# Block two of a four-layer network: another order of projection units, selection rounds and scalings

## The chip, the cores and the metric

The kernel runs on one core of a Trainium2 chip. The metric is the device time of one execution in microseconds (us). TensorE (PE) does the matmuls, VectorE (DVE), ScalarE (ACT) and GpSimd (POOL) the elementwise work, and SyncE (SP) issues the weight loads. Each engine runs its own program in order; they meet only at semaphores.

## The reference

Two blocks of two layers each work on a residual stream of 512 tokens by 1024 channels, in float32. Block one (dilated attention and a gated delta rule, then a convolutional feed-forward) is not touched. A layer of block two computes:

```python
h = rms_norm_2(x, g_pre_mix[l])
u_pool, q, k, v, iq, ik, iw = jnp.split(h @ w_in[l], SPLIT_POINTS, axis=-1)
q, k, iq, ik = ...          # partial rotation (rope) of each
a_out = pool_mixer(u_pool, w_pool[l], pool_scale[l])
b_out = dsa_attention(q, k, v, iq, ik, iw, topk)      # topk = 128
x = x + rms_norm_2(jnp.concatenate([a_out, b_out], -1) @ w_out[l], g_post_mix[l])
h = rms_norm_2(x, g_pre_ffn[l])
x = x + rms_norm_2(jnp.square(jax.nn.relu(h @ w_ff1[l])) @ w_ff2[l], g_post_ffn[l])
```

The pool mixer takes, for four groups of 128 channels, the mean over the last 2, 4, 8 or 16 tokens minus the token itself, multiplies by a 128x128 matrix and scales by a factor per channel. The attention first scores every key for every query: eight index heads give `relu(iq . ik / 8)`, and the score is their sum weighted by `iw`. Only the 128 best keys of a query (among those allowed by 64-token chunks) take part in the softmax attention of eight heads of width 64.

## The kernel before

**Tiling.** Tokens are the free dimension (512), channels the partitions. Weights come as "units" of 128x1024 floats, which is one block of 128 output columns. SP loads a unit into one of two `raw` slots, ACT copies it to `wH` (rounded, `high_of`, line 977), POOL subtracts to get `wL` (`low_of`, line 788), and PE multiplies (`unit`, line 1961): for each of 8 channel tiles three matmuls (high by high, low by high, high by low), 24 matmuls of 128x512. `wH` and `wL` have two slots, so a unit can be prepared once the unit two before it is done.

**The projection stage of block two.** Each layer has `IN2` = 22 places: 0 is `ik`; 1 to 4 are the index queries `iq`; 5 to 8 the four pool groups; 9 and 10 two of the attention's `q` units; place 11 (`WPOOL`) is no unit but the loading of the pool matrices; 12 and 13 are the other two of `q`, 14 to 17 `k`, 18 to 21 `v`. Accumulators alternate between two PSUM banks.

- A unit of `ik`, `iq`, `q` or `k` is "turned" (numbered j = 0 to 12): ACT copies the accumulator out (`turn_input`, line 1083), PE multiplies the copy by a permutation after the next unit's matmuls (`turn`, line 2127), POOL multiplies the copy by the cosines (line 933), and DVE multiplies PE's result by the sines and adds (`turn_finish`, lines 1520 and 1524).
- A unit of `v` (j = 13 to 16) is transposed by PE (line 2131), and DVE scales the result per token into `v2` (line 1528).
- A pool unit is scaled by DVE into `pu` (line 1508), and `pool_window` (lines 1866 to 1875) adds shifted copies of it in one to four doubling steps (2, 4, 8, 16 tokens), partly in SBUF, the last in PSUM bank `SC[1]`, which odd turns use too. ACT and POOL split the result into `pdH` and `pdL` (lines 1018 and 824).
- `pool_mix` (lines 2164 to 2166) multiplies the windows by the pool matrices: groups 0 and 1 at `WPOOL`, 2 and 3 one place later. It writes the banks that odd index pairs use, so it waits until the scores of 14 pairs are taken in. `pool_scaled` on DVE (line 1856) then scales them into `piece`, and ACT and POOL split that.

**Index scores.** Sixteen pairs of heads (128, 256, 384 and 512 keys wide, four pairs each) are spread by `IX_AT` over the places. `index_logits` (line 2115) issues a pair between the channel tiles of a unit, the last pair before the last tile. ACT applies relu in place (line 1330), DVE multiplies by the head's weight and adds into `bias2` (`index_score`, lines 1814 and 1816). There are two sets of two banks, so PE's pair n waits until DVE has taken in pair n-2; pairs 14 and 15 share one set, so 15 waits for 14.

**Selection.** `top_round` finds the eight largest scores of each query and removes them: a MAX8 (line 1830) and a MATCH_REPLACE8 (line 1833) for each token tile, 16 rounds for each of tiles 1, 2 and 3. `TOP_AT` says which rounds run on DVE at the end of which place, `TOP_STEPS` which run between the 35 steps of the attention. A round needs nothing but the scores.

**Attention.** Step n: PE multiplies k by q (line 2222), DVE adds the selection bias and finds the maximum (line 1542), ACT takes the exponential (line 1092), PE transposes (line 2234) one step later. Between them `FILL` puts matmuls of the output projection (`half_step`, lines 2190 to 2192), two steps of three matmuls ahead of every second transposition.

DVE's loop over the places is written out: at place u it does the scaling of a pool unit, the scores of the pairs issued at place u+1, the turn or window of u, and then the rounds of u. ACT's loop: the relus of u, `turn_input`, the weight copy for u+2, then the pieces. POOL's loop: the weight subtraction for u+2, the cosines, then the pieces.

## Time and profile before

| | |
|---|---|
| median of three runs | 2760.77 us (2760.47 to 2763.85) |
| the profiled execution | 2765.85 us, of which the traced span is 2764.1 us |
| PE busy | 2685.1 us, 97% of the span |
| DVE, ACT, POOL busy | 1098.6, 1102.5, 1211.5 us (40, 40, 44%) |
| chain that ended last | PE 87%, DVE 5%, ACT 2%, issue 2%, DVE's sequencer 2%, POOL 1% |
| mean granted clock of TensorE | 0.990 |
| units of block two's first layer, from the turn after place 4 to the turn after place 14 | 1547.09 to 1621.24 us |
| the same of its second layer | 2168.30 to 2243.83 us |

The table reads so: PE is the engine that sets the time, and its idle time in the whole span is 79 us. The projection stage of block two ends, and its attention begins, at 1666 us in the first layer and at 2289 us in the second. What the change can move are the times at which PE waits there.

### The profile page before, as it was taken

To read this page: it belongs to the slowest core of one execution; us is meant where nothing else is said; L and a number is where in the kernel's file an instruction comes from. 1 tells how busy PE (TensorE), PEld (TensorE's weight loads), DVE (VectorE), ACT (ScalarE), POOL (GpSimd) and SP (SyncE) were. 2 spreads that over 40 slices of the span, in tenths; PEclk is the share of its full clock that TensorE was granted. 3 is DMA by queue.
4 is the path that set the end of the run, shared out by engine and by line. 5 is a ranking of instruction groups with operands and counts; after the bars stand their busy time and mean duration, and the time that the engine had idled before them with its cause. 6 is when DMAs were issued, how large, how long until landed. Compare 5 with 4: busy or idle time off the path is not lost.

```text
span 2764.1 us, 42821 instructions
## 1 busy us (share of the span) xinstructions
PE 2685.1 (97%) x15208; PEld 2112.3 (76%) x15208; DVE 1098.6 (40%) x2260; ACT 1102.5 (40%) x1871; POOL 1211.5 (44%) x630
## 2 busy tenths in 40 slices
PE   9999999999999999999999999999999999999997
PEld 7767777888877677788887666788888666788886
DVE  4455454441154553644402586510113586510112
ACT  4454254443345533544434235532333235532331
POOL 3323235555433232355544452464653452364653
PEclk9999999999999999999999999999999999999998
DMA  3211023333322100233232221133332221133332
GB/s 136 77 54 40 9 77 91 99 93 105 106 71 69 54 25 24 78 97 96 94 106 92 71 69 47 62 99 99 92 98 84 71 69 47 61 97 94 99 93 97
DMA packets 62867, 217.16 MB, mean 79 GB/s; under 512 B 6576, under 2 KB 6704, under 8 KB 62480
## 3 DMA queue, kind: packets, MB, share of 16 engines
q1 hardware_dynamic: 62416, 214.28, 24.7%
q8 instruction: 83, 1.36, 0.2%
q0 software_dynamic: 320, 1.12, 0.2%
q14 instruction: 48, 0.39, 0.0%
HBM read 213.28 MB, written 2.10 MB: 78 GB/s over the span
## 4 chain that ended last, share of the span: by engine, by line
PE 87%; DVE 5%; ACT 2%; issue 2%; DVEq 2%; POOL 1%; DMA 0%; ACTq 0%; SPq 0%; POOLq 0%
PE bank L1961 61%; PE bank L2337 3%; PE bank L2011 3%; PE bank L2190 2%; PE bank L2191 2%; PE bank L2192 2%; PE bank L2023 1%; PE bank L2222 1%; PE bank L2234 1%; PE bank L2245 1%; PE bank L2127 1%; PE bank L1995 1%; PE bank L2356 1%; DVE mT L1786 1%; PE bank L1988 1%
## 5 line engine op out<-in xcount | busy, mean ns | idle before, releaser
L788 POOL TENSOR_TENSOR wL<-raw,wH 128x1024 fp32r<-128x1024 f32 x371 | 893.1, 2408 | 1085.5 <-ACT wH L977 1085.4
L1961 PE MATMUL bank<-hH,wH 128*128 128x512 f32 x1680 | 679.8, 405 | 7.0 <-DVE mT L1786 4.2
L1961 PE MATMUL bank<-hL,wH 128*128 128x512 f32 x1680 | 657.9, 392 | 0.0
L1961 PE MATMUL bank<-hH,wL 128*128 128x512 f32 x1680 | 657.5, 391 | 0.0
L977 ACT ACTIVATE wH<-raw 128x1024 fp32r<-128x1024 f32 x371 | 392.2, 1057 | 531.1 <-PE bank L1961 490.8
L1961 PEld LDWEIGHTS bank<-hH,wH 128*128 128x128 f32 x1680 | 317.1, 189 | 102.4 <-issue 28.8
L1961 PEld LDWEIGHTS bank<-hH,wL 128*128 128x128 f32 x1680 | 317.3, 189 | 67.5 <-issue 6.0
L1961 PEld LDWEIGHTS bank<-hL,wH 128*128 128x128 f32 x1680 | 316.9, 189 | 67.8
L1961 PE MATMUL bank<-hidH,wH 128*128 128x512 f32 x864 | 336.7, 390 | 0.0
L1961 PE MATMUL bank<-hidH,wL 128*128 128x512 f32 x864 | 336.2, 389 | 0.0
L1961 PE MATMUL bank<-hidL,wH 128*128 128x512 f32 x864 | 336.1, 389 | 0.0
L1919 DVE SCALAR_TENSOR_TENSOR relu<-bank,rstd 128x512 f32<-128x512 f32 x64 | 44.1, 691 | 458.2 <-PE bank L1961 449.5
L1961 PEld LDWEIGHTS bank<-hidH,wH 128*128 128x128 f32 x864 | 162.2, 188 | 35.8 <-issue 1.6
L1961 PEld LDWEIGHTS bank<-hidL,wH 128*128 128x128 f32 x864 | 162.2, 188 | 33.7
L1961 PEld LDWEIGHTS bank<-hidH,wL 128*128 128x128 f32 x864 | 162.2, 188 | 33.1
L824 POOL TENSOR_TENSOR hidL<-piece,hidH 128x512 f32 (+1 forms) x108 | 139.8, 1295 | 92.8 <-ACT hidH L1018 75.5
L1786 DVE SCALAR_TENSOR_TENSOR mT<-bank,par,mT 128x511 f32<-128x511 f32 (+1 forms) x176 | 131.9, 750 | 115.8 <-ACT mT L1289 101.7
L1092 ACT ACTIVATE sc<-sc,st 128x128 f32<-128x128 f32 (+3 forms) x128 | 71.7, 560 | 109.2 <-DVEq L1545 109.0
L1782 DVE TENSOR_TENSOR bank<-bank,rstd 128x512 f32<-128x512 f32 x88 | 61.5, 698 | 118.2 <-PE bank L1961 110.8
L1463 DVE TENSOR_TENSOR mT<-mT,bank 128x512 f32<-128x512 f32 x42 | 28.9, 687 | 160.5 <-PE bank L1961 128.0
L2190 PE MATMUL bank<-hH,wH 128*128 128x512 f32 (+1 forms) x208 | 81.2, 390 | 1.1 <-POOL hL L824 1.1
L2192 PE MATMUL bank<-hL,wH 128*128 128x512 f32 (+1 forms) x208 | 77.8, 374 | 0.0
(378 smaller groups left out, 3629.9 us busy)
## 6 DMA issues: line engine op xcount, KB each, us to landing
raw<-w_dram SPq DMA_DIRECT2D x398, 512.0 KB, 3.5
x<-x_dram SPq DMA_DIRECT2D x4, 512.0 KB, 9.6
out_dram<-x SPq DMA_DIRECT2D x1, 2048.0 KB, 6.3
const<-const_dram SPq DMA_DIRECT2D x1, 1229.0 KB, 13.2
par_next<-par_dram POOLq DMA_DIRECT2D x5, 168.0 KB, 3.5
qkT<-pos_dram POOLq DMA_DIRECT2D x1, 256.0 KB, 7.3
const<-const_dram SPq DMA_DIRECT2D x1, 131.0 KB, 2.2
```

The lines of the kernel that those rows point to most:

```text
L788: pool.tensor_tensor(wL[:, s, :], raw[:, s, :], wH[:, s, :].bitcast(F32), ALU.subtract).then_inc(w_lo.sem, 1)
L824: pool.tensor_tensor(dst, shape(src), hi.bitcast(F32), ALU.subtract).then_inc(piece_lo.sem, 1)
L977: act.activation(wH[:, s, :], raw[:, s, :], ACT.Copy).then_inc(w_hi.sem, 1)
L1092: act.activation(sc[:, n % 2, 0:wd], sc[:, n % 2, 0:wd], ACT.Exp, bias=st[:, MN + n % 4:MN + n % 4 + 1], scale=-1.0, accum_out=st[:, SUM + ...
L1782: dve.tensor_tensor(banks[s][:, :], banks[s][:, :], rstd[:, :], ALU.mult).then_inc(acc_scaled.sem, 1)
L1786: last = dve.scalar_tensor_tensor(buf[:, lag:S], banks[s][:, 0:S - lag], prmd(w, "fconv", i * 12 + 6 * q + 3 * s + 2 - lag), buf[:, lag:S] ...
L1961: mm = pe.matmul((out or ACC[bk])[:, :], wt[:, c:c + P], rhs, start=first and k == 0 and j == 0, stop=last and k == tiles - 1 and j == 2)
L2011: pe.matmul(out[u][:, :], wt[:, k * P:k * P + P], hH[:, k, :], start=k == 0 and j == 0, stop=False)
L2190: pe.matmul(out[:, cols], wH[:, p % 2, c:c + P], high[:, cols], start=k == 0, stop=False)
L2191: pe.matmul(out[:, cols], wL[:, p % 2, c:c + P], high[:, cols], start=False, stop=False)
L2192: mm = pe.matmul(out[:, cols], wH[:, p % 2, c:c + P], low[:, cols], start=False, stop=k == 3)
L2337: mm = pe.matmul(o, *two, start=True, stop=True)
```

## The change

It renumbers the places of block two. The four pool groups sit at places 5, 7, 9 and 11, between them and at 12 the `q` units (6, 8, 10, 12), and `WPOOL` becomes 13. The sixteen index pairs are dealt two to a place (6 to 12, and 14) where they were 2, 3, 3, 3, 3 and 2 (6 to 10, and 12). The rounds of `TOP_AT` are dealt anew, with the same number for each tile. Scaling the pool results goes from DVE (one instruction and ACT's copy) to ACT (two instructions, one for `piece`, one for `pdH`), and scaling the values goes from DVE (one instruction of 128x512) to ACT (four of 128x128). Odd turns from j = 5 wait for the windows finished up to their place. The SP queue issues the same loads; only their order follows the places.

```diff
@@ -65,14 +65,19 @@
 GROUPS = (28 + 16 + 2 * NJ + KD, 21 + 16 + NH2 + KD * FCHUNKS)
 
 
-WPOOL, IN2, HALF_A, HALF_B, FF_2 = 11, 22, 22, 26, 30
+POOLS = (5, 7, 9, 11)
+WPOOL, IN2, HALF_A, HALF_B, FF_2 = 13, 22, 22, 26, 30
 G_HALF, G_FF2 = (28, 21), 37
 HALF_OF = ((28, 32), (HALF_A, HALF_B))
 
 
 def tensor_of(p):
 
-    return p if p < WPOOL else IN2 - 1 if p == WPOOL else p - 1
+    if p in POOLS:
+        return 5 + POOLS.index(p)
+    if p == WPOOL:
+        return IN2 - 1
+    return p if p < 5 else p - 1 if p > WPOOL else 9 + sum(q < p for q in range(5, p) if q not in POOLS)
 
 
 def group_of(b, u):
@@ -186,15 +191,17 @@
 
 
 IX_AT, _y = {}, 0
-for _u, _n in ((6, 2), (7, 3), (8, 3), (9, 3), (10, 3), (12, 2)):
+for _u, _n in ((6, 2), (7, 2), (8, 2), (9, 2), (10, 2), (11, 2), (12, 2), (14, 2)):
     IX_AT[_u] = tuple(range(_y, _y + _n))
     _y += _n
 assert _y == 16
 
 
-TOP_AT = {10: [[1, 2]], 11: [[1, 2, 3], [1, 2, 3]]}
-for _u in range(12, IN2 - 2):
-    TOP_AT[_u] = [[1, 2, 3]] + ([[1]] if 13 <= _u < 18 else [[2]] if _u >= 18 else [])
+TOP_AT = {9: [[1]], 10: [[1, 2]], 12: [[1, 2]], 13: [[1, 2]], 18: [[1, 2, 3], [1, 2, 3]]}
+for _u in range(14, 18):
+    TOP_AT[_u] = [[1, 2, 3], [1]]
+for _u in (19, 20):
+    TOP_AT[_u] = [[1, 2, 3], [2, 3]]
 TOP_STEPS = {1: [[2]], 3: [[2]], 5: [[3]], 7: [[2]], 9: [[3]], 11: [[3]], 13: [[3]], 15: [[3]], 17: [[3]]}
 _done = {1: 0, 2: 0, 3: 0}
 for _table in (TOP_AT, TOP_STEPS):
@@ -666,13 +673,13 @@
 
             if b == 0:
                 return u if u < 12 else None
-            if u < POOL_U:
-                return u
-            return None if u < POOL_U + 4 or u == WPOOL else u - 4 - (u > WPOOL)
+            if u in POOLS or u == WPOOL:
+                return None
+            return u - sum(p < u for p in (*POOLS, WPOOL))
 
         def unit_of_turn(b, j):
 
-            return j if b == 0 or j < POOL_U else j + 4 + (j + 4 >= WPOOL)
+            return j if b == 0 else [u for u in range(IN2) if turn_of(1, u) is not None][j]
 
         def acc_of(w, u):
 
@@ -932,8 +939,8 @@
                         pool.wait_ge(turn_done.sem, turn_done.at(w, j - 1))
                         pool.tensor_tensor(pt2[:, j % 2, :], turn_src(1, j), rope_r(1)[0],
                                            ALU.mult).then_inc(cos_done.sem, 1)
-                    if 0 < u - POOL_U <= 4:
-                        g = u - POOL_U - 1
+                    if u - 1 in POOLS:
+                        g = POOLS.index(u - 1)
                         piece_low(w, N_PD2 + g, piece[:, g % 2, :], pdL[:, g, :], pdH[:, g, :])
                     if u in (WPOOL + 1, WPOOL + 2):
                         for g in (0, 1) if u == WPOOL + 1 else (2, 3):
@@ -1108,6 +1115,29 @@
                 if w.b and n in HIGHS_AT:
                     f = HIGHS_AT[n]
                     piece_high(w, N_ATT2 + f, piece[:, f % 2, :], att_place(w, f, hH), heads)
+
+            def pool_scaled(w, g):
+
+                if g == 1:
+                    act.wait_ge(unit_done.sem, unit_done.at(w, WPOOL + 1))
+                else:
+                    act.wait_ge(pool_done.sem, pool_done.at(w, (1, 0, 2, 3)[g]))
+                act.wait_ge(piece_ready.sem, piece_ready.at(w, N_PY2 + g))
+                act.wait_ge(piece_lo.sem, piece_lo.at(w, N_PY2 + g - 1))
+                act.activation(piece[:, g % 2, :], MIX[g % 2][:, :], ACT.Copy,
+                               scale=prm(w, "pscale", g, g + 1)).then_inc(piece_ready.sem, 1)
+                act.activation(pdH[:, g, :], MIX[g % 2][:, :], ACT.Copy,
+                               scale=prm(w, "pscale", g, g + 1)).then_inc(piece_hi.sem, 1)
+
+            def value_scaled(w, j):
+
+                f = j - N_ROT[1]
+                act.wait_ge(turn_done.sem, turn_done.at(w, j))
+                act.wait_ge(turned.sem, turned.at(w, j + 1))
+                for t in range(NT):
+                    last = act.activation(v2[:, t, f * P:f * P + P], turned_bank(1, j)[:, t * P:t * P + P], ACT.Copy,
+                                          scale=rtok[:, t:t + 1])
+                last.then_inc(turn_done.sem, 1)
 
             def first_half(w, h):
 
@@ -1336,12 +1366,15 @@
                         high_of(w, 4)
                     elif u >= 3:
                         high_of(w, u + 2)
-                    if 0 < u - POOL_U <= 4:
-                        g = u - POOL_U - 1
+                    if u - 1 in POOLS:
+                        g = POOLS.index(u - 1)
                         piece_high(w, N_PD2 + g, piece[:, g % 2, :], pdH[:, g, :])
-                    if u in (WPOOL + 1, WPOOL + 2):
-                        for g in (0, 1) if u == WPOOL + 1 else (2, 3):
-                            piece_high(w, N_PY2 + g, piece[:, g % 2, :], pdH[:, g, :])
+                    if u in (WPOOL, WPOOL + 1):
+                        for g in (0, 1) if u == WPOOL else (2, 3):
+                            pool_scaled(w, g)
+                    if u and (turn_of(1, u - 1) or 0) >= N_ROT[1]:
+                        value_scaled(w, turn_of(1, u - 1))
+                value_scaled(w, turn_of(1, IN2 - 1))
                 for n in range(SLOTS):
                     for h in HALVES_AT[n - 1] if n else ():
                         first_half(w, h)
@@ -1846,16 +1879,6 @@
                                   8 ** -0.5, None, ALU.mult)
                 dve.drain()
 
-            def pool_scaled(w, g):
-
-                if g == 1:
-                    dve.wait_ge(unit_done.sem, unit_done.at(w, WPOOL + 1))
-                else:
-                    dve.wait_ge(pool_done.sem, pool_done.at(w, (1, 0, 2, 3)[g]))
-                new_piece(w, N_PY2 + g)
-                dve.tensor_scalar(piece[:, g % 2, :], MIX[g % 2][:, :], prm(w, "pscale", g, g + 1), None,
-                                  ALU.mult).then_inc(piece_ready.sem, 1)
-
             def pool_window(w, g):
 
                 win = 2 << g
@@ -1886,20 +1909,14 @@
                         gate_scale(w)
                     j = turn_of(1, u)
                     if j is None and u != WPOOL:
-                        unit_scaled(w, u, pu[:, (u - POOL_U) % 2, :], acc_free[u % 2].sem)
+                        unit_scaled(w, u, pu[:, POOLS.index(u) % 2, :], acc_free[u % 2].sem)
                         dve.drain()
-                    if u == WPOOL:
-                        for g in (0, 1):
-                            pool_scaled(w, g)
                     for y in (2 * pair + h for pair in IX_AT.get(u + 1, ()) for h in range(2)):
                         index_score(w, y)
-                    if j is not None:
+                    if j is not None and j < N_ROT[1]:
                         turn_finish(w, j)
-                    elif u != WPOOL:
-                        pool_window(w, u - POOL_U)
-                    if u == WPOOL + 1:
-                        for g in (2, 3):
-                            pool_scaled(w, g)
+                    elif j is None and u != WPOOL:
+                        pool_window(w, POOLS.index(u))
                     for rounds in TOP_AT.get(u, ()):
                         top_round(rounds)
                 for n in range(SLOTS):
@@ -2119,8 +2136,9 @@
                 src, to = turn_src(w.b, j), turned_bank(w.b, j)
                 bk, a = acc_of(w, unit_of_turn(w.b, j))
                 pe.wait_ge(acc_free[bk].sem, acc_free[bk].at(w, a + 1))
-                if w.b and j == POOL_U:
-                    pe.wait_ge(piece_ready.sem, piece_ready.at(w, N_PD2 + 4))
+                if w.b and POOL_U <= j < 15 and j % 2:
+                    windows = sum(p < unit_of_turn(1, j) for p in POOLS)
+                    pe.wait_ge(piece_ready.sem, piece_ready.at(w, N_PD2 + windows))
                 if w.b and j == 15:
                     pe.wait_ge(ix_used.sem, ix_used.at(w, 32))
                 if j < N_ROT[w.b]:
@@ -2159,7 +2177,7 @@
                     pe.wait_ge(ix_used.sem, ix_used.at(w, 28))
                 pe.wait_ge(piece_lo.sem, piece_lo.at(w, N_PD2 + g + 1))
                 if g >= 2:
-                    pe.wait_ge(piece_ready.sem, piece_ready.at(w, N_PY2 + g - 1))
+                    pe.wait_ge(piece_hi.sem, piece_hi.at(w, N_PY2 + g - 1))
                 c = g * P
                 pe.matmul(MIX[g % 2][:, :], pwH[:, c:c + P], pdH[:, g, :], start=True, stop=False)
                 pe.matmul(MIX[g % 2][:, :], pwL[:, c:c + P], pdH[:, g, :], start=False, stop=False)
```

## Rows read from the trace of the kernel before

**Rows 1.** the page: busy time of each engine, share of the span.

```profile
PE 2685.1 (97%) x15208; PEld 2112.3 (76%) x15208; DVE 1098.6 (40%) x2260; ACT 1102.5 (40%) x1871; POOL 1211.5 (44%) x630
```

**Rows 2.** stretches: length, PE PEld DVE ACT POOL busy, clock, DMA share, GB/s.

```profile
1547.00:1609.00 62.00, 55.41 (x227) 34.64 (x226) 46.50 (x86) 22.26 (x47) 24.28 (x13) 0.97 0.21 67
...
1582.00:1588.00 6.00, 6.00 (x20) 4.06 (x18) 5.59 (x9) 1.31 (x3) 3.36 (x2) 0.72 0.23 79
```

**Rows 3.** PE's waits, each layer of block two: total, times, longest.

```profile
PE bank L2115 <- DVE bias L1816: 5.8, 4, 2.0
...
PE bank L2115 <- DVE bias L1816: 7.4, 4, 2.8
```

**Rows 4.** timeline of PE, first layer: start, length, instruction, idle before.

```profile
1547.09 1.02 PE L2127 MATMUL bank<-turn_in,const 128*128 128x512 f32 x2
...
1580.39 0.92 PE L2115 MATMUL bank<-ikT,iqT 64*128 64x384 f32 x4 [2.04 <-DVE bias L1816]
...
1595.72 0.47 PE L2164 MATMUL bank<-pdH,pwH 128*128 128x512 f32 x1 [0.76 <-issue]
...
1606.20 1.13 PE L2115 MATMUL bank<-ikT,iqT 64*128 64x512 f32 x4 [1.62 <-DVE bias L1816]
...
1621.24 1.02 PE L2127 MATMUL bank<-turn_in,const 128*128 128x512 f32 x2
```

**Rows 5.** timeline of PE, second layer.

```profile
2168.30 1.02 PE L2127 MATMUL bank<-turn_in,const 128*128 128x512 f32 x2
...
2213.29 1.88 PE L2115 MATMUL bank<-ikT,iqT 64*128 64x512 f32 x4 [2.78 <-DVE bias L1816]
...
2243.83 1.02 PE L2127 MATMUL bank<-turn_in,const 128*128 128x512 f32 x2
```

**Rows 6.** timeline, a DVE window step and a POOL instruction beside it.

```profile
1573.25 2.65 DVE L1866 TENSOR_TENSOR sc<-sc 128x510 f32<-128x510 f32 x1
...
1572.69 2.66 POOL L788 TENSOR_TENSOR wL<-raw,wH 128x1024 fp32r<-128x1024 f32 x1 [2.91 <-ACT wH L977]
```

**Rows 7.** DVE's groups by shape, 1540 to 1670 us: busy, mean ns.

```profile
L1816 DVE SCALAR_TENSOR_TENSOR bias<-bank,iw,bias 128x512 f32<-128x512 f32 x7 | 5.2, 750 | 2.3 <-ACT bank L1330 1.8
...
L1866 DVE TENSOR_TENSOR sc<-pu 128x511 f32<-128x511 f32 x3 | 2.1, 692 | 0.3
```

**Rows 8.** ACT's groups by shape, the same stretch.

```profile
L1018 ACT ACTIVATE pdH<-piece 128x512 fp32r<-128x512 f32 x8 | 5.0, 634 | 20.8 <-DVEq L1876 18.4 <-DVE piece L1856 2.3
...
L1330 ACT ACTIVATE bank<-bank 128x512 f32<-128x512 f32 x8 | 4.3, 577 | 9.0 <-PE bank L2115 9.0
```

**Rows 9.** timeline of PE, end of the projection and start of the attention.

```profile
1646.55 1.02 PE L2127 MATMUL bank<-turn_in,const 128*128 128x512 f32 x2
...
1666.15 0.49 PE L2222 MATMUL bank<-kT,qT 64*128 64x128 f32 x4
...
1668.07 0.27 PE L2234 MATMUL bank<-const,sc 128*128 128x128 f32 x1
```

**Rows 10.** timeline of DVE, rounds of the selection and the first softmax step.

```profile
1601.11 0.89 DVE L1830 MAX8 top<-bias 128x8 f32<-128x256 f32 x2
...
1603.24 1.41 DVE L1856 TENSOR_SCALAR piece<-bank,par 128x512 f32<-128x512 f32 x2
...
1649.16 1.48 DVE L1830 MAX8 top<-bias 128x8 f32<-128x256 f32 x3
...
1652.47 0.43 DVE L1830 MAX8 top<-bias 128x8 f32<-128x256 f32 x1
...
1653.53 0.69 DVE L1528 TENSOR_TENSOR v<-bank,rtok 128x512 f32<-128x512 f32 x1
...
1657.43 0.56 DVE L1830 MAX8 top<-bias 128x8 f32<-128x384 f32 x1
...
1666.88 0.29 DVE L1542 CUSTOM_DVE_ANT_0 sc<-bank,bias 128x128 f32<-128x128 f32 x1
```

**Rows 11.** timeline of ACT, the first exponential of the attention.

```profile
1667.25 0.40 ACT L1092 ACTIVATE sc<-sc,st 128x128 f32<-128x128 f32 x1 [0.80 <-DVEq L1545]
```

## The prediction

> **What bounds the kernel now.** First the page: PE is busy for 97% of the span [rows 1], so only PE's waits and its slow clock can be given back. Then the table of stretches [rows 2]: in the first layer's stretch with the pools and index scores (1547 to 1609 us) PE is busy 55.4 of 62 us at a granted clock of 0.97. The waits name the cause [rows 3]: PE waits for DVE's index scores four times a layer, 5.8 and 7.4 us. The timeline shows where [rows 4, 5]: at the third pair of a place (2.04 and 2.78 us) and at pair 15 (1.62 us). Right after the 2.04 us wait the granted clock is 0.72 for 6 us [rows 2], part of it at the lower of the two levels: (1-0.72) x 6 = 1.7 us lost. The 512 wide pair after the wait of 2.78 us takes 1.88 us instead of the 1.13 of another [rows 4, 5]. With the 0.76 us ahead of the first pool matmul [rows 4] and 0.1 at each restart, some 8.5 us are lost in the first layer (5.8 + 0.8 + 1.7), and 1.4 more in the second, by the lengths of the same work: 2243.83-2168.30 = 75.5 against 1621.24-1547.09 = 74.15 us. That is all that the reordering can give: some 18 us.
>
> **Stage A, places 5 to 14.** The work on PE is the same, so I follow the engines from the turn after place 4 (time 0). A place with its turn takes PE (1646.55-1621.24)/4 = 6.33 us [rows 4, 9], without it about 5.4 (the turn's 1.02 overlaps by 0.1), an index pair its duration and about 0.15. With two pairs a place no pair but 15 has to wait for the pair two before it: four waits a layer become one. But DVE gets a full queue. From place 10 on it holds, in order: the scores of pairs 8 and 9 (done at 39.1), the third window, one round of tile 1, the scores of 10 and 11, a round of two tiles (1603.24-1601.11 = 2.1 us [rows 10]), the finish of a turn (two of 0.69 and drains, 1.6), the scaling of the last pool group (0.8), the scores of pairs 12 and 13 (four of 0.75, 0.83 with their gaps [rows 7]).
>
> How long a window takes hangs on POOL. A step of a window adds two SBUF operands: 0.69 us alone [rows 7], 2.65 us where POOL's weight subtraction runs [rows 6]. The third window is 3.5 us clean (four operations and the ends), the fourth 4.35. In the new order each falls on a subtraction of 2.4 us and a cosine product of 1.3, which follow a `q` unit at once. I add 3.5 us to the third and 2.5 to the fourth (bounds: 0 and 3.7 each, all of both POOL instructions). The third then ends at 46.3, 0.8 us after PE wants it for its odd turn; DVE reaches pairs 12 and 13 at 54.85 and ends them at 58.15, while PE ends place 12 at 55.2: it waits 3 us ahead of the pool matmuls, where it waited 0.8. (If the third window takes 5.5 us, 2.2.)
>
> Next wait: pair 15, issued in place 14. The fourth window ends at 65.1. ACT has stood waiting for it and then does its piece (0.63 [rows 8]), the weight copy for place 15 (1.06), and the new scalings of two pool groups, four instructions at a pitch of about 0.5 (the relu of the same 512 columns is 0.58 [rows 8]); only then comes the relu of pair 14, and DVE adds two products of 0.83. Sum: 65.1 + 0.1 + 0.6 + 1.0 + 2.0 + 0.6 + 1.6 = 71.0. PE wants pair 15 at 66.6: 4.5 us of waiting, where it was 1.62. PE ends place 14 at 73.05. The same work (one turn more, two pool matmul groups less, 0.5 us) was done before at 1621.24-1547.09-0.5 = 73.65 us in the first layer and 2243.83-2168.30-0.5 = 75.05 in the second [rows 4, 5]. One low-clock stretch of up to 1.65 us after the long wait is to be added, so stage A gives -0.6 to +1.0 and -2.0 to -0.4: I take -1 us for both layers. With clean windows pair 15 comes 2.5 to 4 us earlier, -4 a layer; with POOL's full block +1.5.
>
> The rule for the block is in the Trainium skill, SBUF — State Buffer, section Who interferes with whom: a VectorE instruction with two SBUF inputs and a GpSimd instruction that reads SBUF exclude each other for the whole instruction, whichever comes first. The pair at 1573 us agrees: DVE 2.65 us, POOL 2.66 where it mostly takes 2.4. By the rule both POOL instructions hold the window up, which leads to the -1; if only running beside each other slowed them a little, it would be -4 a layer.
>
> **Stage B, the start of the attention.** The rounds are the same in number, but not in place. Before, DVE has at places 18 and 19 a three-tile and a one-tile round each; after, place 18 has two three-tile rounds, 19 and 20 each a three-tile and a two-tile one. None waits for anything, so DVE goes through them without a pause after the last `k` turn, and the attention's first step stands behind them. Durations [rows 10]: three tiles 1652.47-1649.16 = 3.3 us, tile 1 alone 1653.53-1652.47 = 1.06, tile 2 alone 1.28 (0.56, 0.54 and gaps), tiles 2 and 3 about 2.5 (three tiles less tile 1's 0.8). From DVE's start on place 17's rounds (1649.16, which is 2.6 us after PE's turn at 1646.55 [rows 9]): 4.35 for place 17, 6.6 for 18, 5.8 for 19, 5.8 for 20, and 0.6 to close tile 1 = 23.15 us, so DVE is free at 1672.3. The first softmax step was at 1666.88 [rows 10]: DVE is 5.4 us late. PE had 0.4 us of slack at its first transposition (1668.07 [rows 9], the exponential from 1667.25 to 1667.65 [rows 11]), and has nothing to fill with but the two steps already there; DVE's selection round behind step 1 takes away the rest of the slack. I take 5.4 us a layer (bounds: 4.9, if DVE works off the lag in its gaps, and 5.7). It cannot be shortened by PE's gain in stage A, since it counts from a turn that moves along.
>
> The wait is longer than any of [rows 4, 5], so a stretch at the low clock should follow: 0 to 1.7 us a layer by [rows 2], I take 1.2.
>
> The values: four ACT instructions of 128x128 a unit, about 0.85 us, instead of 0.69 on DVE. After the last unit ACT does a copy of its input, a weight copy and eight of these, some 3.4 us, until its first exponential. That hides behind DVE's lag; without the lag it would cost some 0.9 us a layer (from 1667.25, the first exponential, to 1668.1). ACT's doubled pool scalings delay place 17's weights to some 0.8 us before PE wants them: hidden, but nothing is left over. The waits of odd turns for four windows are met by then, and the SP queue brings each load a place earlier than needed: zero.
>
> **Sum.** -1 + 2 x 5.4 + 2 x 1.2 = +12.2 us. The profiled execution took 2765.85 us with a span of 2764.1; the median is 5.1 lower, 2760.77. I put the difference on the median: 2773.0 us.
>
> **Rivals.**
> 1. Stage A pays for stage B (no change). If the windows run clean, A gives -4 to -5 a layer and no low clock follows B: 2760.8 - 9 + 10.8 = 2762.6. For it: the windows at places 5 and 7 mostly fall between POOL's instructions. Against: the third and fourth start within a subtraction by my schedule. 0.13.
> 2. Faster: the third-pair waits go and nothing takes their place. Place and price: the 8.5 and 9.9 us of stage A less what remains of pair 15 (1.6 each): 2745.6. It decides at the point where the rounds of places 18 to 20 end: it needs them inside 17.7 us from 1649.16, and I count 23.15. 0.04; in between, a half of both (2755 or less) 0.03.
> 3. Slower still: POOL blocks all of both windows, the lag passes to the weights behind ACT's scalings (place 17 and 18, 1 us each), and each long wait has its low clock: 2760.8 + 3 + 10.8 + 6.8 = 2781. 0.13.
> 4. The moved scalings on ACT decide, not DVE's rounds: then PE's first waits of the attention name ACT's exponential after ACT's own queue, and the time is 2760.8 - 1 + 2 = 2762, within the same as rival 1. 0.03.
>
> The forecast holds 0.64. Its own range is 2767 to 2779; rivals 1 and 4 at 2762 and rival 3 near 2781 lie at the edges, so the range is 2763 to 2780. A measurement of this kernel can tell from no change what is over 0.2%, 5.5 us: slower (over 2766.3) 0.77, within 0.16 (rivals 1 and 4), faster 0.07 (rival 2).
>
> **What would show it.** In the profile after: no wait of PE for index scores in places 7 to 11; 2 to 3 us of waiting ahead of the first pool matmul and 2.5 to 5 at pair 15, behind ACT's pool scalings; one wait of about 5 us in each layer at the attention's first transposition, with DVE busy on MAX8 and MATCH_REPLACE8 until some 25.7 us after the last `k` turn; then a stretch of 0.6 us matmuls. The prediction is wrong if DVE reaches the first softmax step within a microsecond of PE's first product, or if stage A gains over 5 us a layer.

## The result, and the profile after

The changed kernel takes 2782.88 us (median of 5 runs, 2778.95 to 2788.58) against 2762.91 for the kernel before, measured alongside (2760.47 to 2767.95): ratio 1.0071, interval 1.006 to 1.0082. It is slower by 20.0 us. The forecast was 12.2 us more, 2773.0, in a range from 2763 to 2780: the direction is right, the step is 7.8 us too short and the time lies 2.9 us above the range.

The profiled execution took 2788.58 us, with a span of 2786.8, so 22.7 us more of span than before. It is the slowest of the five: 5.7 us above their median, at a mean granted clock of 0.985 where the other four have 0.987 to 0.989. What its rows say of the clock is therefore more than a usual execution loses. Its totals, against [rows 1] (busy time, share of the span, instructions):

```profile
span 2786.8 us, 42861 instructions
PE 2698.0 (97%) x15208; PEld 2121.7 (76%) x15208; DVE 1094.0 (39%) x2244; ACT 1116.8 (40%) x1911; POOL 1211.9 (43%) x630
```

The same 15208 matmuls are busy for 13 us more, at a mean granted clock of 0.985 where it was 0.990. The rest, some 10 us, is waiting. PE's waits over the whole span (total, times, longest):

```profile
PE bank L2252 <- ACT turn_in L1114: 11.0, 6, 2.6
PE bank L2252 <- ACT sc L1099: 10.8, 2, 5.6
...
PE bank L2182 <- issue: 5.6, 2, 2.8
PE bank L2132 <- DVE bias L1849: 4.6, 2, 2.3
```

The index-score waits of [rows 3], 13.2 us in 8 places, are down to 4.6 in 2. In their place stand two waits of 2.8 ahead of the pool matmuls (L2182) and two of over 5 us at the attention's first transposition (L2252 behind ACT's exponential, L1099). Where the 22.7 us are, by the timeline of PE (start, length, instruction, what it waited for; rows of both layers, compare [rows 4, 5, 9]):

```profile
1547.64 1.02 PE L2145 MATMUL bank<-turn_in,const 128*128 128x512 f32 x2
...
1593.61 1.10 PE L2145 MATMUL bank<-turn_in,const 128*128 128x512 f32 x2 [0.28 <-DVEq L1899]
...
1605.53 0.47 PE L2182 MATMUL bank<-pdH,pwH 128*128 128x512 f32 x1 [2.79 <-issue]
...
1618.04 1.13 PE L2132 MATMUL bank<-ikT,iqT 64*128 64x512 f32 x4 [2.30 <-DVE bias L1849]
...
1665.37 0.49 PE L2240 MATMUL bank<-kT,qT 64*128 64x128 f32 x4
...
1672.71 0.48 PE L2252 MATMUL bank<-const,sc 128*128 128x128 f32 x1 [5.26 <-ACT sc L1099]
...
1691.30 0.41 PE L2252 MATMUL bank<-const,sc 128*128 128x128 f32 x2 [2.60 <-ACT turn_in L1114]
...
2180.29 1.02 PE L2145 MATMUL bank<-turn_in,const 128*128 128x512 f32 x2
...
2299.53 0.49 PE L2240 MATMUL bank<-kT,qT 64*128 64x128 f32 x4
...
2307.20 0.47 PE L2252 MATMUL bank<-const,sc 128*128 128x128 f32 x1 [5.58 <-ACT sc L1099]
```

From the turn after place 4 to the attention's first product the first layer takes 1665.37-1547.64 = 117.73 us where it took 1666.15-1547.09 = 119.06 [rows 4, 9]; the second layer 119.24 where it took 120.44. That stage gives 2.5 us. From the first product of the attention to the first matmul of the norm's sum behind it, the times of the same two instructions are 105.31 and 103.86 us; before, they were 91.04 and 92.58. That stage costs 14.3 + 11.3 = 25.6 us. The two account for the span: 25.6 - 2.5 = 23.1. Stage A by itself scatters more than its gain: warm and close_early below, with the same code up to there, took 2.9 us more and 0.2 more in the first layer than this execution, and the same in the second.

Stretches of 50 us that hold the first half of the attention, first after, then before (length, busy time of PE, PEld, DVE, ACT and POOL, granted clock, DMA share, GB/s), and of the first layer after the first product in steps of 10 us:

```profile
1664.00:1714.00 50.00, 39.87 (x215) 26.30 (x215) 33.73 (x129) 23.23 (x72) 8.43 (x4) 0.83 0.13 42
...
2298.00:2348.00 50.00, 39.52 (x223) 26.00 (x221) 34.24 (x133) 24.59 (x76) 8.45 (x4) 0.86 0.13 42
...
1664.00:1674.00 10.00, 4.49 (x25) 2.90 (x23) 9.03 (x30) 4.99 (x15) 2.40 (x1) 0.89 0.29 100
1674.00:1684.00 10.00, 9.54 (x36) 6.45 (x37) 4.49 (x23) 3.35 (x13) 0.00 (x0) 0.59 0.00 0
1684.00:1694.00 10.00, 7.38 (x43) 4.82 (x42) 8.04 (x28) 4.85 (x16) 2.37 (x1) 0.92 0.18 53
1694.00:1704.00 10.00, 8.46 (x49) 5.59 (x48) 5.91 (x23) 4.86 (x17) 1.28 (x1) 0.84 0.01 2
```

```profile
1664.00:1714.00 50.00, 46.62 (x314) 31.18 (x314) 32.25 (x139) 30.98 (x89) 12.22 (x6) 1.00 0.14 43
...
2288.00:2338.00 50.00, 46.72 (x304) 31.13 (x305) 30.94 (x136) 30.37 (x89) 12.21 (x6) 0.97 0.11 39
```

The granted clock is 0.83 and 0.86 over 50 us, where it was 1.00 and 0.97. (1-0.83) x 50 = 8.5 and (1-0.86) x 50 = 7.0 us bound what that can cost, where the bounds were 0 and 1.5; PE was idle for 10 of the 50 us, so the cost is less. From 1674 to 1684, behind the wait of 5.26, the clock is 0.59, and in the twenty microseconds behind these it is below 1.00 still.

The same matmuls, timed from the attention's first product, divide the 25.6 us without that bound (us, before and after):

| | first layer | second layer |
|---|---|---|
| first transposition begins | 1.92, 7.34 | 1.91, 7.67 |
| from there to the matmul behind the closing of tile 2 | 12.71, 18.59 | 12.71, 18.63 |
| of this, PE's wait ahead of that matmul | 0.27, 2.60 | 0.27, 2.52 |
| from there to the norm's sum | 76.41, 79.38 | 77.96, 77.56 |

(The closing of a tile is the TENSOR_SCALAR that DVE runs behind the tile's last selection round; it turns the scores into the attention's bias.) So the late rounds cost 5.4 + 5.8 = 11.2 us, the wait behind the closing 2.3 + 2.25 = 4.6, and the rest, 6.5 + 3.3 = 9.8 us, goes with matmuls that take longer: in the first layer's attention PE is busy for 92.9 us where it was 85.8, at a mean granted clock of 0.92 where it was 1.00.

Why PE waits at 1667 shows on DVE (timeline; compare [rows 10]):

```profile
1668.54 0.29 DVE L1871 TENSOR_SCALAR bias<-bias 128x256 f32<-128x256 f32 x1
...
1669.13 1.16 DVE L1863 MAX8 top<-bias 128x8 f32<-128x384 f32 x2
...
1670.96 0.68 DVE L1866 MATCH_REPLACE8 bias<-top,bias 128x512 f32<-128x512 f32 x1
...
1671.78 0.29 DVE L1575 CUSTOM_DVE_ANT_0 sc<-bank,bias 128x128 f32<-128x128 f32 x1
```

DVE works on the selection without a gap until 1671.6; the first softmax starts at 1671.78, ACT's exponential at 1672.16 (it was 1667.25 [rows 11]).

And why PE waits again, at 1691, DVE and POOL in the same kernel:

```profile
1686.90 2.54 DVE L1871 TENSOR_SCALAR bias<-bias 128x384 f32<-128x384 f32 x1
...
1686.85 2.37 POOL L795 TENSOR_TENSOR wL<-raw,wH 128x1024 fp32r<-128x1024 f32 x1 [18.71 <-ACT wH L984]
```

This is the closing of tile 2. It came 0.05 us behind the start of POOL's subtraction and ended 0.22 us after it. In the kernel before the pair came in the other order, and PE's wait at the same matmul was short:

```profile
1678.56 0.36 DVE L1838 TENSOR_SCALAR bias<-bias 128x384 f32<-128x384 f32 x1
...
1678.66 2.50 POOL L788 TENSOR_TENSOR wL<-raw,wH 128x1024 fp32r<-128x1024 f32 x1 [9.73 <-ACT wH L977]
...
1680.78 0.41 PE L2234 MATMUL bank<-const,sc 128*128 128x128 f32 x2 [0.27 <-ACT turn_in L1107]
```

2.54 against 0.36 us, and PE's wait behind it is 2.60 where it was 0.27. By the Trainium skill, SBUF — State Buffer, section Who interferes with whom, `copy` and `tensor_scalar` can, if their operands meet its conditions, enter a mode that takes the port pair DVE shares with GpSimd, and whoever issues first holds it for the whole instruction. The rows of both orders agree. So does the second layer: DVE's closing came 0.55 us behind the start of the subtraction, took 2.05, and ended 0.22 us after it as well; PE waited 2.52.

### The profile page after: what moved, and what is told of

Its sections match the earlier page's. It is cut to its first block, busy times and chain, and to the rows that moved or that the text cites. A ratio compares the mean times of both kernels' runs of the same rounds, so it can differ in the third digit from the quotient of the medians.

```text
span 2786.8 us, 42861 instructions
## 1 busy us (share of the span) xinstructions
PE 2698.0 (97%) x15208; PEld 2121.7 (76%) x15208; DVE 1094.0 (39%) x2244; ACT 1116.8 (40%) x1911; POOL 1211.9 (43%) x630
## 4 chain that ended last, share of the span: by engine, by line
PE 87%; DVE 6%; ACT 2%; issue 2%; DVEq 2%; POOL 1%; DMA 0%; ACTq 0%; SPq 0%; POOLq 0%
PE bank L1978 60%; PE bank L2028 3%; PE bank L2355 3%; PE bank L2208 2%; PE bank L2210 2%; PE bank L2209 2%; PE bank L2040 1%; PE bank L2240 1%; PE bank L2252 1%; PE bank L2263 1%; PE bank L2145 1%; PE bank L2012 1%; DVE bias L1866 1%; PE bank L2132 1%; PE bank L2374 1%
## 5 line engine op out<-in xcount | busy, mean ns | idle before, releaser
L831 POOL TENSOR_TENSOR hidL<-piece,hidH 128x512 f32 (+1 forms) x108 | 139.9, 1296 | 92.9 <-ACT hidH L1025 75.4
L1099 ACT ACTIVATE sc<-sc,st 128x128 f32<-128x128 f32 (+3 forms) x128 | 71.7, 560 | 120.2 <-DVEq L1578 119.9
L2252 PE MATMUL bank<-const,sc 128*128 128x128 f32 x320 | 60.9, 289 | 25.0 <-ACT turn_in L1114 11.0
```

Of the source, the lines that this page charges most:

```text
L831: pool.tensor_tensor(dst, shape(src), hi.bitcast(F32), ALU.subtract).then_inc(piece_lo.sem, 1)
L1099: act.activation(sc[:, n % 2, 0:wd], sc[:, n % 2, 0:wd], ACT.Exp, bias=st[:, MN + n % 4:MN + n % 4 + 1], scale=-1.0, accum_out=st[:, SUM + ...
L2252: tr = pe.transpose(PT[:, j * P:j * P + P], sc[:, m % 2, j * P:j * P + P], ident)
```

## The experiments

The theory from this profile: (a) the late selection rounds make the first wait, (b) that wait brings a long stretch at the low clock, (c) a closing of a tile that meets POOL's subtraction makes a second wait, (d) the scalings moved to ACT cost little. The rival is that ACT's new work, or the new order of the places itself, carries the loss. "Stage A" is the time from the first product of index pair 0 to the attention's first product, "attention" that from there to the norm's first sum, both in the profiled execution, first and second layer. Before: stage A 114.0 and 115.4, attention 91.0 and 92.6; after: 112.7 and 114.2, 105.3 and 103.9. Differences of times are between medians of different sets of executions; the kernel before, measured beside each set, had medians from 2762.91 to 2763.92, so a microsecond of such a difference is not to be trusted.

**The rounds alone.** The kernel before, with only the late table of rounds:

```diff
-TOP_AT = {10: [[1, 2]], 11: [[1, 2, 3], [1, 2, 3]]}
-for _u in range(12, IN2 - 2):
-    TOP_AT[_u] = [[1, 2, 3]] + ([[1]] if 13 <= _u < 18 else [[2]] if _u >= 18 else [])
+TOP_AT = {10: [[1]], 11: [[1, 2]], 12: [[1, 2]], 13: [[1, 2]], 18: [[1, 2, 3], [1, 2, 3]]}
+for _u in range(14, 18):
+    TOP_AT[_u] = [[1, 2, 3], [1]]
+for _u in (19, 20):
+    TOP_AT[_u] = [[1, 2, 3], [2, 3]]
```

> The kernel before with nothing changed but the places of the rounds: the late dealing of the changed kernel. Values are still scaled on VectorE, four instructions of 0.7 us more in its queue, so it comes 5.4 + 2.8 = 8.2 us late to the attention's first step. Theory: a wait of about 8 us a layer, the low clock behind it and a second wait, 13 to 17 us a layer: 2789 to 2797 us. Rival (it is the other edits, the order of the units and ScalarE's scalings, that cost): under 2770 us.

Measured: 2788.92 us, ratio 1.0091 (1.0077 to 1.0105); attention 102.3 and 100.4. PE's timeline at the place:

```profile
1673.62 0.48 PE L2236 MATMUL bank<-const,sc 128*128 128x128 f32 x1 [7.62 <-ACT sc L1094]
```

The rounds alone cost 25.0 us, where the whole change costs 20.0 (the intervals of the ratios overlap). So (a) holds; that the other parts give some 5 us back is likely, not shown. The wait is 7.6 in both layers where the full change has 5.3 and 5.6: here DVE also scales the values (four of 0.69 a layer, 2.8 us), which the change gives to ACT. The second wait that was expected did not come: the six closings took 0.29 to 0.43 us, and the two of tile 2 came 0.10 us ahead of POOL's subtraction. The profiled execution is the fastest of its five, 2780.74, 8 us below their median, so its attention shows less than the 25 us.

**The rounds early, in the changed kernel.** Only the table differs from after:

```diff
-TOP_AT = {9: [[1]], 10: [[1, 2]], 12: [[1, 2]], 13: [[1, 2]], 18: [[1, 2, 3], [1, 2, 3]]}
-for _u in range(14, 18):
+TOP_AT = {9: [[1]], 10: [[1, 2]], 12: [[1, 2]], 13: [[1, 2, 3], [2, 3]], 14: [[1, 2, 3], [1, 2]],
+          18: [[1, 2, 3], [1, 2, 3]], 19: [[1, 2, 3]], 20: [[1, 2, 3]]}
+for _u in range(15, 18):
     TOP_AT[_u] = [[1, 2, 3], [1]]
-for _u in (19, 20):
-    TOP_AT[_u] = [[1, 2, 3], [2, 3]]
```

> The changed kernel with only the rounds of the selection dealt anew, the same rounds in the same number: the pause that VectorE has in place 13 takes two rounds more, place 14 one, and places 19 and 20 keep one round of three tiles each. From the last k turn VectorE then has 4.35 + 6.6 + 3.3 + 3.3 + 0.6 = 18.15 us of rounds where the attention gives it 17.7. Theory (the queue of rounds is what costs): the wait of 5.3 us at the first transposition falls under 0.6 us, the low clock after it and the later wait of 2.6 us go too, and what is left is stage A's gain of 1.3 us a layer: 2760.4 us, 0.992 of the changed kernel. Rival (ScalarE's value scalings hold the first exponential up): a wait of 1 us or more stays there, 2763 to 2766 us. Second rival (the loss lies in stage A and its waits): 2775 us or more.

Measured: 2772.16 us (7 runs), ratio 1.0031 (1.002 to 1.0043): 10.7 us less than after, and 12 above the 2760.4 expected. Attention 99.3 and 93.3. DVE, POOL and PE at the start of the attention:

```profile
1665.06 2.31 DVE L1870 TENSOR_SCALAR bias<-bias 128x256 f32<-128x256 f32 x1
...
1664.84 2.38 POOL L794 TENSOR_TENSOR wL<-raw,wH 128x1024 fp32r<-128x1024 f32 x1 [3.52 <-ACT wH L983]
...
1668.67 0.33 PE L2251 MATMUL bank<-const,sc 128*128 128x128 f32 x1 [2.13 <-ACT sc L1098]
...
1686.01 0.41 PE L2251 MATMUL bank<-const,sc 128*128 128x128 f32 x2 [2.52 <-ACT turn_in L1113]
```

Now the closing of tile 1 meets the subtraction: 2.31 us, in both layers, where after took 0.29, and PE waits 2.13 at both first transpositions. The closing of tile 2 took 2.39 in the first layer, with the wait of 2.52 behind it, and 0.36 in the second, where it began 0.01 us behind the start of the subtraction and was not held. So three closings of four met POOL, and (c) took back about 2 us each time.

**The low clock alone.** After, with 22 products of 128x128 into a bank that nobody reads, ahead of the first transposition, in the gap in which PE waited:

```diff
                 m = n - 1
                 if 0 <= m < 32:
                     f, i, h = att_step(m)
+                if w.b and m == 0:
+                    keep_warm(STAT, 22)
```

> The changed kernel with 22 small matmuls (128x128, into a bank that nobody reads) put before the attention's first transposition in block two, so that TensorE works while it waits for the late rounds, some 4.7 us. Theory (half of the loss is the low clock that follows an idle TensorE): the first wait shrinks to under 1 us, no stretch at the low clock follows, 4 to 7 us a layer come back: 2769 to 2775 us. Rival (the loss is the wait and nothing else): no change, 2783 us, or slower by what the matmuls overrun.

Measured: 2776.67 us, ratio 1.0046 (1.0033 to 1.006), 6.2 less than after and 1.7 above the range expected: 3 us a layer came back, not 4 to 7. Attention 96.3 and 100.0. Stretches in each layer:

```profile
1666.00:1686.00 20.00, 18.69 (x126) 14.37 (x124) 16.28 (x67) 10.64 (x36) 3.28 (x2) 1.00 0.16 50
2311.00:2321.00 10.00, 7.41 (x42) 4.62 (x40) 6.16 (x21) 4.29 (x15) 1.97 (x1) 0.83 0.17 52
```

The fill does not move the first transposition: it begins 7.35 and 7.67 us after the first product, as in after. In the first layer the clock is 1.00 where it was 0.59, the closing of tile 2 came 0.10 us ahead of POOL's subtraction (0.36 us), and 96.3 is the 91.0 of before plus 5.3, the late start itself. So of the first layer's 14.3 us the late start is 5.4, and 9.0 is what came after it: (b) and (c) together, 6.5 and 2.3 by the table above. In the second layer the clock was 1.00 from 2300 to 2310, and 3.9 us came back up to the matmul behind the closing, whose wait (2.59 at 2315.03) stayed: there the gain is (b) alone. Behind that wait the clock is 0.83; a low stretch does not need a wait of 5 us.

**The closing alone.** After, with the last round of tile 2 two steps earlier:

```diff
-TOP_STEPS = {1: [[2]], 3: [[2]], 5: [[3]], 7: [[2]], 9: [[3]], ...
+TOP_STEPS = {1: [[2]], 3: [[2]], 5: [[2]], 7: [[3]], 9: [[3]], ...
```

> The changed kernel with two steps of the selection swapped inside the attention: tile 2 gets its last round and is closed at step 5, tile 3 gets its round at step 7. The closing instruction (0.36 us alone) took 2.54 us at step 7, where it met GpSimd's weight subtraction. Theory: this collision is worth 2.2 us a layer and the low clock behind it, 2 to 4 us a layer: 2775 to 2779 us, and the wait of 2.6 us is gone. Rival (another wait takes its place at once, since VectorE is late anyway): within 1 us of the changed kernel.

Measured: 2778.11 us, ratio 1.0058 (1.0044 to 1.0072): 4.8 less than after, with overlapping intervals. Attention 99.7 and 101.9. PE's waits, the closings (shortest, median, longest, ns), and the stretch of 50 us:

```profile
PE bank L2252 <- ACT sc L1099: 10.9, 2, 5.6
PE bank L2252 <- ACT turn_in L1114: 6.4, 4, 1.6
...
L1871 DVE TENSOR_SCALAR bias<-bias x6: 293/361/428, 1667.1 to 2336.1; 128x256 f32<-128x256 f32 x2, 128x384 f32<-128x384 f32 x2, 128x512 f32<-128x512 f32 x2
...
1664.00:1714.00 50.00, 41.32 (x252) 27.33 (x252) 33.32 (x139) 26.74 (x85) 9.70 (x5) 0.93 0.10 33
```

The first wait is as before this edit, and the 2.6 is gone. 4.8 us less in the time fits the 2.33 and 2.25 us by which that wait had grown in the two layers. The clock is a second thing: behind the same wait, 5.27, it is 0.93 over the 50 us where after has 0.83 (0.83 from 1671 to 1681, where after has 0.50 from 1672 to 1682). So the wait alone does not say how long the low clock lasts.

**Rounds early and closings clear.** rounds_early with one round of tile 2 in place 20 where it had a round of all three tiles, a round of tile 1 more in place 19, tile 2 closed in step 5 and one more round of tile 3 in step 19:

```diff
-          18: [[1, 2, 3], [1, 2, 3]], 19: [[1, 2, 3]], 20: [[1, 2, 3]]}
+          18: [[1, 2, 3], [1, 2, 3]], 19: [[1, 2, 3], [1]], 20: [[2]]}
-TOP_STEPS = {..., 5: [[3]], 7: [[2]], ..., 17: [[3]]}
+TOP_STEPS = {..., 5: [[2]], 7: [[3]], ..., 17: [[3]], 19: [[3]]}
```

> The changed kernel with the rounds dealt so that they end in time and none of the closings meets GpSimd: as in the first early dealing, but tile 1 closes in place 19 (there it took 2.31 us in place 20, beside GpSimd's weight subtraction), place 20 keeps one round of tile 2, tile 2 closes at step 5 of the attention, and one round of tile 3 moves from place 20 to step 19. Theory (late rounds, the closings that wait for the shared port, and the low clock behind them are the whole loss in the attention): the attention takes 91 to 93 us from its first product to the sum of the squares, as before the change, where it took 99.3 and 93.3 with the first early dealing; the time is 2760 to 2764 us. Rival (ScalarE's eight value scalings ahead of the first exponential hold it too): a wait of 0.6 us or more stays at the first transposition and the time is over 2765 us.

Measured: 2766.73 us (12 runs), ratio 1.0014 (1.0006 to 1.0023). Attention 95.5 and 93.7: of the 25.6 us that the attention had lost, 20 are back; in the medians it is 16 of 20. The forecast, 2760 to 2764, was missed by 3, and its rival came true: ACT's value scalings hold the first exponential up, with a wait of over 0.6 and a time over 2765. What is left shows in ACT's and PE's timelines:

```profile
1665.45 2.30 ACT L1137 ACTIVATE v<-bank,rtok 128x128 f32<-128x128 f32 x8
1667.62 0.41 ACT L1098 ACTIVATE sc<-sc,st 128x128 f32<-128x128 f32 x1
...
1668.18 0.33 PE L2251 MATMUL bank<-const,sc 128*128 128x128 f32 x1 [0.87 <-ACT sc L1098]
...
1707.71 0.52 PE L2251 MATMUL bank<-const,sc 128*128 128x128 f32 x3 [2.06 <-ACT turn_in L1113]
```

DVE's two softmax steps were done by 1666.6. The exponential waited for ACT's own eight value scalings, which the prediction had named as hidden behind DVE's lag. The 2.06 us are the round put into step 19, with tile 3's closing behind it.

**ACT's pool scalings undone.** After, with the four pool results scaled on DVE as before and rounded on ACT:

```diff
-                    if u in (WPOOL, WPOOL + 1):
-                        for g in (0, 1) if u == WPOOL else (2, 3):
-                            pool_scaled(w, g)
+                    if u in (WPOOL + 1, WPOOL + 2):
+                        for g in (0, 1) if u == WPOOL + 1 else (2, 3):
+                            piece_high(w, N_PY2 + g, piece[:, g % 2, :], pdH[:, g, :])
```

> The changed kernel with the scaling of the pool results put back on VectorE (one instruction a group, ScalarE only splits it), nothing else undone. Theory (ScalarE's four scalings between the fourth window and the relu of pair 14 are only one of two queues of like length: VectorE has a turn, a round of two tiles and now two scalings there): the wait at pair 15 stays between 2 and 4 us and the time within 3 us of the changed kernel, 2780 to 2786 us. Rival (ScalarE's scalings alone make pair 15 late, as the prediction's sum had it): the wait falls under 1 us, 2779 us or less.

Measured: 2784.94 us, ratio 1.0082 (1.0069 to 1.0095), 2.1 above after, with overlapping intervals: ACT's pool scalings do not carry the loss, and (d) holds for the pool results. The first wait grows from 5.3 and 5.6 to 6.0 in both layers, and pair 15 waits 4.7 and 2.6. The comparison is not clean: in the profiled execution both closings of tile 2 came 0.10 us ahead of POOL's subtraction (0.36 us), so it lacks the 4.6 us of (c). If its other executions are like it, the scalings on DVE cost more than the 2.1 us that show.

**The relu first.** rounds_early_2, with ACT's relu of pair 14 ahead of the pool scalings 0 and 1, not behind them:

```diff
+                        if y == 29:
+                            for g in (0, 1):
+                                pool_scaled(w, g)
...
-                    if u in (WPOOL, WPOOL + 1):
-                        for g in (0, 1) if u == WPOOL else (2, 3):
+                    if u == WPOOL + 1:
+                        for g in (2, 3):
                             pool_scaled(w, g)
```

> The second early dealing, with ScalarE's order changed in place 14: the relu of pair 14 goes ahead of the scalings of pool groups 0 and 1 and not behind them. Theory: pair 14's scores are ready 2.3 us earlier, the wait at pair 15 (2.3 to 4.0 us) goes to under 1 us, 1.5 to 3.5 us a layer come back: 2755 to 2760 us, faster than both kernels. Rival (VectorE's queue, turn and round, sets it anyway): within 1 us of the second early dealing.

Measured: 2765.15 us (11 runs), ratio 1.0009 (1.0001 to 1.0018), 5 above the range expected and 1.6 below rounds_early_2, with overlapping intervals. The wait at pair 15 is 1.63 in the first layer and 2.0 in the second, where it was 2.3 and 2.5: ACT's order was worth some 0.6 us of it. That the rest is the relu, DVE's two products and the distance to the fourth window is read from the order of the work, not tried.

**The same, with products in the gap ahead of the pool matmuls.** `keep_warm(ACC[1], 12)` in front of the first:

> The same with 12 small matmuls into a free bank ahead of the first pool matmul, so that TensorE is busy in its wait of 2.8 us there. Theory (an idle TensorE is followed by a stretch at the low clock in some executions): 0 to 1.6 us a layer less than without, 2754 to 2759 us, and a granted clock of 1.00 through places 12 to 14. Rival: no difference, the low stretches come all the same.

Measured: 2766.2 us (9 runs), ratio 1.0015 (1.0005 to 1.0024), where 2754 to 2759 was expected: no gain. The 2.8 us are filled, no low clock follows them, and pair 15 waits 3.3 in both layers. values_later_close below, without the fill, waits 3.3 there too, in both layers, since its clock stayed at 1.00 up to pair 15; relu_first, whose clock was low between the two places, waits 1.63 and 2.0. So a slow stretch of PE ahead of pair 15 only shortens the wait there, and what PE doesn't lose at the first place it loses at the next. That the fourth window sets the time of both is argued, not tried.

**The values behind the first exponentials.** relu_first, with the scaling of the last unit's values behind the second attention step in ACT's order:

```diff
-                value_scaled(w, turn_of(1, IN2 - 1))
                 for n in range(SLOTS):
                     for h in HALVES_AT[n - 1] if n else ():
                         first_half(w, h)
                     attention(w, n)
+                    if n == 1 and w.b:
+                        value_scaled(w, turn_of(1, IN2 - 1))
```

> relu_first with one edit: ScalarE scales the values of the last turn behind the exponential of the second attention step, not ahead of the first one. In rounds_early_2 the first softmax was ready on VectorE at 1666.6, ScalarE was busy with eight value scalings until 1667.6, its first exponential ran at 1667.62, and TensorE waited 0.87 at the first transposition; relu_first has the same wait (0.87). Theory (the rest of that wait is ScalarE's queue): first transposition waits 0 to 0.3 in both layers, and the time is 0.6 to 0.8 a layer below relu_first's 2765.2: 2763.6. Rival (it is VectorE's selection rounds alone): the wait stays at 0.8 and the time at 2765.

Measured: 2763.79 us (11 runs), ratio 1.0001 (0.9992 to 1.001), near the 2763.6 expected; the interval overlaps that of relu_first. ACT:

```profile
1662.93 1.14 ACT L1137 ACTIVATE v<-bank,rtok 128x128 f32<-128x128 f32 x4
1663.93 0.43 ACT L1098 ACTIVATE sc<-sc,st 128x128 f32<-128x128 f32 x1
...
1665.13 1.14 ACT L1137 ACTIVATE v<-bank,rtok 128x128 f32<-128x128 f32 x4
```

No wait is left at the first transposition, where relu_first had 0.87; attention 92.9 and 92.7.

**And tile 3 closed in step 17 again.**

```diff
-TOP_STEPS = {..., 13: [[3]], 15: [[3]], 17: [[3]], 19: [[3]]}
+TOP_STEPS = {..., 12: [[3]], 13: [[3]], 15: [[3]], 17: [[3]]}
```

> values_later with one edit: the selection round of tile 3 that stood in attention step 19 (with the closing of that tile, 2.1 us of VectorE ahead of two softmaxes, and a TensorE wait of 2.06 behind it in rounds_early_2 and relu_first) stands in step 12, so that the tile closes in step 17, as in the kernel before. Theory (each late closing is a wait of TensorE's own, about 2 us, and brings a 0.83 clock after it): the wait of 2.06 goes, 2 to 3.5 us less over the two layers than values_later, about 2761. Rival (the round costs the same wait wherever it stands in attention): a wait of 1.5 to 2 appears near step 12 and the time is unchanged, 2763 to 2764.

Measured: 2761.66 us (11 runs, 2760.23 to 2764.89), ratio 0.9994 (0.9985 to 1.0003). The 2.06 is gone, a wait of 0.91 for a softmax step came near step 12; attention 92.4 and 92.2. PE's waits:

```profile
PE bank L2255 <- ACT turn_in L1113: 6.6, 5, 1.6
PE bank L2135 <- DVE bias L1852: 6.6, 2, 3.3
```

This version has the new order of places and the scalings on ACT, two of them at another point of ACT's order, and is 21 us faster than the changed kernel, yet it can't be told from the kernel before. So neither the order nor ACT's new work carries the loss. Its stage A, 113.5 in both layers against 114.0 and 115.4, puts the new order at 1.2 us a layer, by one execution of each; the three executions with the changed kernel's own stage A (after, warm, close_early) average 113.9, 0.8 below the kernel before.

## Why the prediction went as it did

**Stage A was right in its mechanism and near in size.** Predicted -1 us for both layers together, in the profile -2.5, and some -1.5 by the three executions just named. Times from the turn after place 4, predicted and measured in the first layer: end of the third window 46.3, 45.8; the wait of the odd turn 0.8, 0.28; ahead of the pool matmuls 3.0, 2.79; the third pool matmul group 73.05, 72.27. The one large miss is pair 15, 4.5 forecast and 2.30 and 2.33 measured. PE wanted it at 68.1, not at 66.6, and the fourth window ended 0.8 earlier. POOL did block the windows, as the sum had it: a step of 2.70 and a copy of two columns of 1.25 in the third, steps of 1.87 and 1.53 in the fourth, where 0.69 is the clean length [rows 7]:

```profile
1587.65 2.70 DVE L1889 TENSOR_TENSOR sc<-sc 128x510 f32<-128x510 f32 x1
1590.27 1.25 DVE L1890 COPY sc<-sc 128x2 f32<-128x2 f32 x1
...
1605.52 1.87 DVE L1889 TENSOR_TENSOR sc<-pu 128x511 f32<-128x511 f32 x1
...
1607.53 1.53 DVE L1889 TENSOR_TENSOR sc<-sc 128x510 f32<-128x510 f32 x1
```

The windows took 6.6 and 6.4 us for the 7.0 and 6.85 of the sum. Rivals 1 and 2, which needed clean windows or no new wait, fall with these rows.

**Stage B's wait was right.** 5.4 us forecast; the first transposition began 5.4 and 5.8 us later than before (PE's waits of 5.26 and 5.58), by the mechanism named. The attention started 0.8 us earlier than before, so DVE's forecast 1672.3 becomes 1671.5, and it was 1671.78. The run with the rounds alone shows it as the cause.

**The step that failed is the term for what follows that wait: 1.2 us a layer.** The prediction wrote "0 to 1.7 us a layer by [rows 2], I take 1.2". In the profiled execution the attention lost 8.9 us in the first layer and 5.5 in the second beside the late start. Two things are in this.

The closing of tile 2 was put at nothing. The shift of DVE's work by 5 us against POOL's let it fall behind a subtraction: PE's wait at that matmul was 2.60 and 2.52 us where it was 0.27, 4.6 us over both layers, and taking the collision away gave 4.8 in the time (the run with the closing alone). The prediction treated POOL's block for the windows of stage A only.

The low clock was mis-sized. It cost 6.5 us in the first layer; in the second, 4.8 from the first transposition on, where it had cost 1.5 before, so 3.3 more. That is the slowest of five executions; for the median the estimate is 20.0 + 2.5 - 11.2 - 4.6 = 6.7 us for both layers, against 2.4 forecast. The bound of 1.7 came from one wait of 2.04 us, followed by matmuls of the projection, in one execution. Behind the wait of 5.26 the matmuls ran at a clock of 0.59 although PE was busy for 9.54 of the ten microseconds, and it was still at 0.84 from 1694 to 1704. Why the low stretch is long in one execution and short in another stays open: the run with the closing alone has 0.93 over the 50 us behind the same wait, and the rounds alone, with a wait of 7.6, have 0.90.

Together: 4.6 for the closing and 4.3 for the clock, 0.4 for the late start, less 1.5 in stage A, make the 7.8 us by which the step was short. Rival 3, 2781, had a low clock of 6.8 over both layers and is the nearest in time, but its other term, 3 us more of stage A and late weights, did not occur, and it lacks the closing: its time came out near by luck.

**The values on ACT** were hidden behind DVE's lag, as written, and cost 0.87 a layer once the lag was gone, forecast 0.9. They also take 2.8 us from DVE ahead of the attention: with the late rounds alone, where DVE still does them, the wait is 7.6, 2.0 to 2.4 longer. The pool scalings ran at a pitch of 0.57 where 0.5 was assumed, 0.3 us over four.

Settled by runs: the rounds as the cause of the first wait; that filling the gap keeps the clock at 1.00 behind it (both layers, one profiled execution); that the wait of 2.6 goes with the closing; ACT's values and the round in step 19. How much of the loss is clock in a usual execution is an estimate. Only read from the timeline, and not tried with the windows moved: that POOL's block of the windows sets the wait ahead of the pool matmuls.

## What to carry to other kernels

When work of an engine off the critical path is dealt out anew, add up its queue from the last point where it waits to the first instruction that the critical engine needs from it; here DVE had 5.4 us of rounds more than there was room for, and dealing them earlier, with the closings clear of POOL, gave 16 us back, more than the 8.6 us of index-score waits that the change removed. Price a new wait of TensorE by what follows it as well: here the low clock behind the waits of 5.3 and 5.6 us cost 6.5 and 4.8 us in one execution, and less in others. And after a shift, look which short instructions now start beside the other engine's long ones; a tenth of a microsecond decided between 0.36 and 2.5 us.

## What the runs showed of the hardware

- The granted clock was 0.59 for ten microseconds behind a wait of 5.26 us, with PE busy for 9.54 of them. Taken over ten microseconds from the first transposition on, it was 0.50 there, which is the lower of its two levels (1.2 of 2.4 GHz) throughout, 0.83 behind the same wait of 5.27 in close_early, and 0.75 behind one of 7.62 with the rounds alone. From 1704 to 1714 it was 0.83, behind a wait of 2.06, in one run, while the same wait of 2.07 at the same place of another left it at 1.00. Stretches of relu_first, then of values_later:

```profile
1704.00:1714.00 10.00, 10.00 (x64) 6.64 (x63) 3.05 (x15) 6.13 (x15) 3.66 (x2) 0.83 0.01 2
```

```profile
1704.00:1714.00 10.00, 9.88 (x72) 6.52 (x72) 3.26 (x16) 7.55 (x18) 3.68 (x2) 1.00 0.04 13
```

  What decides between the two stays open. It is one source of the scatter between runs of one kernel: of the five of the changed kernel the fastest, 2778.95, has the highest mean clock, 0.989, and the slowest, 2788.58, the lowest, 0.985.
- A one-input TENSOR_SCALAR from SBUF to SBUF took 0.29 to 0.43 us alone, 0.36 when it began 0.10 us ahead of a POOL subtraction, and 2.05 to 2.54 when it began 0.05 to 0.55 us behind the start of one. MAX8 and MATCH_REPLACE8 took the same 0.41 to 0.69 us beside POOL's subtractions as without them.
